# Eleven projection pairs in two transformer blocks: twelve half gates ahead of the pairs, the angle operations in three pairs, stores at the stage heads, transposes ahead of the last gate

## The reference

```python
h = modulate(rms_norm(x, g_pre_mix[l]), shift_m, scale_m)
proj = h @ w_in[l]
q_a, k_a, v_a, q_m, k_m, v_m, o_m, i_m, f_m, g_a, g_m = jnp.split(proj, split_points, axis=-1)
q_a = rope(q_a.reshape(B, S, N_Q_HEADS, HEAD_DIM), positions)
k_a = rope(k_a.reshape(B, S, N_KV_HEADS, HEAD_DIM), positions)
...
qk_m = jax.nn.silu(causal_depthwise_conv(jnp.concatenate([q_m, k_m], axis=-1), conv_w[l], conv_b[l]))
...
h_m = mlstm_chunkwise(q_m, k_m, v_m, i_pre, f_pre)
...
merged = jax.nn.sigmoid(g_a) * (y_a @ w_branch_attn[l]) + jax.nn.sigmoid(g_m) * (y_m @ w_branch_mlstm[l])
```

## Time and profile before

| what | us |
|---|---|
| median of 3 runs | 2745.44 (2743.47 to 2746.28) |
| the profiled execution, its own time | 2742.76 |
| its span (what the profile shows) | 2740.7 |
| PE busy in the span | 2645.3 |
| POOL busy, DVE busy, ACT busy | 1819.3, 1891.0, 1059.6 |
| mean granted TensorE clock, of full speed | 0.992 |

### The profile page before, as it was taken

The page is one execution under the profiler, slowest core; times in us unless marked ns, Lnnn a source line. Parts: engine busy times, 40 slices in busy tenths (PEclk is TensorE's granted clock), DMA queues, the critical chain, the costliest instruction groups (busy, mean ns, idle before and its releaser), DMA issues.

```text
span 2740.7 us, 39654 instructions
## 1 busy us (share of the span) xinstructions
PE 2645.3 (97%) x12718; PEld 2101.6 (77%) x12718; DVE 1891.0 (69%) x2671; ACT 1059.6 (39%) x2141; POOL 1819.3 (66%) x1389
## 2 busy tenths in 40 slices
PE   7999999899999999999899999999999999999998
PEld 5777777677788888877677787777887888888887
DVE  6666687738888888887776463485547667667667
ACT  5555444535534333333433233555234322222222
POOL 4555511357798888876679973222368898888874
PEclk9999999999999999999999999999999999999999
DMA  4322222034211111123422434222444111111133
GB/s 148 104 85 85 92 94 62 16 123 150 78 58 54 54 55 54 55 99 132 161 96 93 123 112 177 78 73 86 152 159 142 46 58 55 56 55 54 58 127 139
DMA packets 98697, 253.55 MB, mean 93 GB/s; under 512 B 9423, under 2 KB 13296, under 8 KB 98292
## 3 DMA queue, kind: packets, MB, share of 16 engines
q1 hardware_dynamic: 72464, 186.41, 21.2%
q10 hardware_dynamic: 26084, 65.21, 6.6%
HBM read 211.20 MB, written 37.77 MB: 91 GB/s over the span
## 4 chain that ended last, share of the span: by engine, by line
PE 82%; DVE 11%; ACT 3%; issue 3%; DMA 0%; ACTq 0%; POOL 0%; POOLq 0%; DVEq 0%; SPq 0%
PE ps L1260 9%; PE ps L1262 9%; PE ps L1261 9%; PE ps L1630 8%; PE ps L1632 8%; PE ps L1631 8%; PE ps L1677 4%; PE ps L1679 4%; PE ps L1678 4%; PE ps L1351 3%; PE ps L1841 2%; PE ps L1843 2%; PE ps L1842 2%; PE ps L1367 2%; PE ps L1937 1%
## 5 line engine op out<-in xcount | busy, mean ns | idle before, releaser
L935 POOL CAST wh<-raw 128x1024 fp32r<-128x1024 f32 x139 | 149.9, 1078 | 584.6 <-PE ps L1262 532.1
L1260 PE MATMUL ps<-hh,wh 128*128 128x512 f32 x1040 | 437.4, 421 | 22.7 <-DVE hl L3230 11.2
L1262 PE MATMUL ps<-hh,wl 128*128 128x512 f32 x1040 | 410.0, 394 | 0.0
L1261 PE MATMUL ps<-hl,wh 128*128 128x512 f32 x1040 | 408.5, 393 | 0.0
L937 POOL TENSOR_TENSOR wl<-raw,wh 128x1024 fp32r<-128x1024 f32 x139 | 336.0, 2417 | 11.1
L1050 POOL TENSOR_TENSOR wl<-raw,wh 128x512 fp32r<-128x512 f32 x156 | 212.7, 1378 | 72.5 <-ACT wh L2442 72.0
L1260 PEld LDWEIGHTS ps<-hh,wh 128*128 128x128 f32 x1040 | 197.3, 190 | 79.8 <-issue 15.0
L1262 PEld LDWEIGHTS ps<-hh,wl 128*128 128x128 f32 x1040 | 196.4, 189 | 43.6
L1261 PEld LDWEIGHTS ps<-hl,wh 128*128 128x128 f32 x1040 | 197.6, 190 | 35.8 <-issue 3.4
L3595 DVE TENSOR_TENSOR hlf<-ps,hlf 128x512 f32<-128x512 f32 x252 | 171.5, 691 | 23.9 <-PE ps L1679 21.7
L1631 PE MATMUL ps<-al,wh 128*128 128x512 f32 x476 | 185.2, 389 | 0.0
(11 more groups left out here) (463 smaller groups left out, 7289.3 us busy)
## 6 DMA issues: line engine op xcount, KB each, us to landing
raw<-weights SPq DMA_DIRECT2D x149, 512.0 KB, 3.6
raw<-weights SPq DMA_DIRECT2D x240, 256.0 KB, 2.6
arena<-w_ada SPq DMA_DIRECT2D x48, 512.0 KB, 3.8
arena<-gate_scratch ACTq DMA_DIRECT2D x25, 512.0 KB, 5.1
gate_scratch<-arena ACTq DMA_DIRECT2D x14, 512.0 KB, 2.8
gate_scratch<-sums_f ACTq DMA_DIRECT2D x17, 256.0 KB, 2.0
arena<-x_t ACTq DMA_DIRECT2D x1, 4096.0 KB, 14.2
x_scratch<-arena ACTq DMA_DIRECT2D x2, 2048.0 KB, 9.1
```

The source lines that it names most:

```text
L1260: pe.matmul(out, wh[:, slot, w], xh, start=start, stop=False)
L1261: pe.matmul(out, wh[:, slot, w], xl, start=False, stop=False)
L1262: return pe.matmul(out, wl[:, slot, w], xh, start=False, stop=stop)
```

## The change

`N_EARLY` becomes 12: one gate half moves from behind the pairs to ahead of them, with its strip, its chunk of weights and its split; strips 8 to 11 use the other half of their tiles and so wait for no earlier store. In pair 0, block 0 now comes before the first half of the rows. The positions are loaded behind the weights of pair 1 instead of ahead of them. POOL waits for all low parts of the activation sums before it starts the weights of pair 1. The angle operations are spread over pairs 1, 2 and 3, and ACT's two sines stand at the end of stage 4. `rope_store` of a pair's first tile stands at the head of its stage. Behind the pairs three gate halves are left; the stabilizer columns follow the first and use banks 5 and 4, all 40 transposes follow the second with three pairs of banks instead of two, and the third gate half comes last. ACT's load of `NEGMB` and its copies of the stabilizer columns are issued earlier, and the last eviction lies inside the recurrence's first step.

```diff
-N_QKV, N_WO, N_FFN, N_PROJ, N_GATE, N_EARLY, N_BR, N_OUT = 24, 14, 3 * NJ + 10, 23, 16, 11, 8, 16
+N_QKV, N_WO, N_FFN, N_PROJ, N_GATE, N_EARLY, N_BR, N_OUT = 24, 14, 3 * NJ + 10, 23, 16, 12, 8, 16
...
+        VT_BANKS = ((0, 1), (2, 3), (6, 5), (0, 1), (2, 3))
...
                 weights(C_PR + 1)
-                sp.wait_ge(Z.n_lo, 48)
-                sp.wait_ge(Z.gs5, 16 * N_EARLY)
-                sp.dma_start(TURNS.bitcast(I32), A.positions).then_inc(Z.pos_in, 16)
                 for j in range(1, N_PAIRS):
...
                     pr_load(j, 1, 1)
+                    if j == 1:
+                        sp.wait_ge(Z.n_lo, 48)
+                        sp.wait_ge(Z.gs5, 16 * N_EARLY)
+                        sp.dma_start(TURNS.bitcast(I32), A.positions).then_inc(Z.pos_in, 16)
...
                 direct_low(0, 6, 0, b22)
+                pool.wait_ge(R.px_lo, PR_LOWS + 16)
                 for j in range(1, N_PAIRS):
...
                     pe.wait_ge(Z.g_ev, N_EARLY - 2)
+                    projection_block(j, 0, b, True)
+                    pe.wait_ge(Z.g_ev, N_EARLY)
                     rows_half(0)
-                    pe.wait_ge(Z.g_ev, N_EARLY)
-                    projection_block(j, 0, b, True)
                     pe.wait_ge(Z.n_lo, 48)
                     rows_half(1)
...
-                if m == N_EARLY + 1:
+                if m == N_EARLY:
+                    stabilizer_columns()
+                elif m == N_EARLY + 1:
                     pe.wait_ge(R.v_back, 16 * 5)
                     pe.wait_ge(Z.if_ev, N_PROJ - 1)
                     v_transposes(0)
                     pe.wait_ge(Z.if_ev, N_PROJ)
                     v_transposes(1)
-                elif m == N_EARLY + 2:
-                    v_transposes(2)
-                    v_transposes(3)
-            v_transposes(4)
-            stabilizer_columns()
+                    pe.wait_ge(Z.g_ev, N_EARLY + 1)
+                    pe.wait_ge(Z.m_tpc, 2)
+                    for n in range(2, 5):
+                        v_transposes(n)
             pe.wait_ge(Z.v_cp, 10)
...
             def projection_stage(j):
 
+                rope_store(j - 2, 0)
                 if j:
                     projection_out(j - 1, 0)
                 projection_copy(j)
                 if j:
                     projection_out(j - 1, 1)
                 projection_cast(j, 2)
-                rope_store(j - 2, 0)
                 row_steps(j)
-                if j == 4:
-                    act.wait_ge(Z.trig, 14)
-                    act.activation(SIN, SIN, ACT.Sin, scale=col("sgn")).then_inc(Z.trig_sin, 1)
-                    act.activation(COS, COS, ACT.Sin).then_inc(Z.trig_sin, 1)
...
                 rope_store(j - 2, 1)
+                if j == 4:
+                    act.wait_ge(Z.trig, 14)
...
+            act.wait_ge(Z.m_row, 16)
+            act.wait_ge(Z.cv_done, 6)
+            act.dma_start(NEGMB, bass.AP(m_dram.tensor, 0, [[0, P], [S, HD_ML], [1, S]])).then_inc(Z.m_mb, 16)
             projection_end(N_PAIRS - 1, 0)
             projection_end(N_PAIRS - 1, 1)
...
+            late_out(N_EARLY)
+            act.wait_ge(Z.m_tp, 4)
+            act.activation(GT, bank(5)[:, 0:32], ACT.Copy).then_inc(Z.m_tpc, 1)
+            act.activation(EMT, bank(4)[:, 0:32], ACT.Copy).then_inc(Z.m_tpc, 1)
+            late_out(N_EARLY + 1)
...
                 projection_add(j, bank(b + 3), bank(b + 2), PR_SUM7, 4, 2)
                 rope_turn(j - 1, 0)
+                if j == 1:
+                    angle_start()
+                elif j == 2:
+                    angle_whole()
+                elif j == 3:
+                    angle_turns(0.25)
                 projection_add(j, bank(b + 1), bank(b + 1), PR_SUM, 5, None)
+                if j == 1:
+                    angle_turns(0.0)
+                elif j == 2:
+                    angle_part(SIN, C1, ANGLE)
+                elif j == 3:
+                    angle_whole()
                 projection_add(j, bank(b + 2), bank(b + 2), PR_SUM, 6, 3)
...
-                if j == 2:
-                    angles(SIN, 0.0)
-                if j == 3:
-                    angles(COS, 0.25)
+                angle_steps(j)
```

More of the change, by code:

```diff
@@ L447, in taps_done @@
             return T_CV[-1] * group + T_CV[2 * u + p]
-        E_STRIPS = [T(m % 8)[:, 0:HALF] for m in range(N_EARLY)]
+        E_STRIPS = [T(m % 8)[:, m // 8 * HALF:(m // 8 + 1) * HALF] for m in range(N_EARLY)]
         E_BANKS = (7, 0, 1, 4)
@@ L1476, in v_transposes @@
                 for half in range(2):
-                    if n >= 2:
-                        pe.wait_ge(Z.v_cp, 2 * (n - 2) + half + 1)
+                    if n >= 3:
+                        pe.wait_ge(Z.v_cp, 2 * (n - 3) + half + 1)
                     for b in range(4):
                         t = slice(half * HALF + b * P, half * HALF + (b + 1) * P)
-                        last = pe.transpose(bank(2 * (n % 2) + half)[:, b * P:(b + 1) * P], V_BACK[n][:, t], mat("ident"))
+                        last = pe.transpose(bank(VT_BANKS[n][half])[:, b * P:(b + 1) * P], V_BACK[n][:, t], mat("ident"))
                     last.then_inc(Z.vT, 1)
@@ L1886, in stabilizer_columns @@
                 pe.wait_ge(Z.if_act, 4)
-                pe.wait_ge(Z.v_cp, 8)
                 for b in range(NB):
-                    pe.matmul(bank(2)[:, b * 4:b * 4 + 4], ROW1[0:4, b * P:(b + 1) * P], mat("ident")[0:4, 0:4],
+                    pe.matmul(bank(5)[:, b * 4:b * 4 + 4], ROW1[0:4, b * P:(b + 1) * P], mat("ident")[0:4, 0:4],
                               start=True, stop=True)
-                    last = pe.matmul(bank(3)[:, b * 4:b * 4 + 4], ROW2[32:36, b * P:(b + 1) * P],
+                    last = pe.matmul(bank(4)[:, b * 4:b * 4 + 4], ROW2[32:36, b * P:(b + 1) * P],
                                      mat("ident")[32:36, 32:36], start=True, stop=True)
@@ L2849, in projection_stage @@
                 rope_store(j - 2, 1)
+                if j == 4:
+                    act.wait_ge(Z.trig, 14)
+                    act.activation(SIN, SIN, ACT.Sin, scale=col("sgn")).then_inc(Z.trig_sin, 1)
+                    act.activation(COS, COS, ACT.Sin).then_inc(Z.trig_sin, 1)
             projection_copy(0)
@@ L2868, in _, with late_out @@
             act.preload_act_table_set("natural_log_exp_and_others")
-            for m in range(N_EARLY, N_GATE - 1):
-                strip_out = (Z.gs0, Z.gs1, Z.gs2, Z.gs3)[m - N_EARLY]
+            def late_out(m):
+                i = m - N_EARLY
                 act.wait_ge(Z.chunk_done, C_GATE0 + m + 1)
-                if m == N_EARLY + 2:
+                if i == 2:
                     act.wait_ge(Z.cv_done, 5)
-                act.activation(G_STRIPS[m - N_EARLY], bank(G_BANKS[m - N_EARLY]), ACT.Copy).then_inc(Z.g_ev, 1)
+                act.activation(G_STRIPS[i], bank(G_BANKS[i]), ACT.Copy).then_inc(Z.g_ev, 1)
                 act.wait_ge(Z.g_ev, m + 1)
-                act.dma_start(sg_dram[HD_ML + m][:, half_of(0)], G_STRIPS[m - N_EARLY]).then_inc(strip_out, 16)
-                if m == N_EARLY:
-                    act.wait_ge(Z.m_row, 16)
-                    act.wait_ge(Z.cv_done, 6)
-                    act.dma_start(NEGMB, bass.AP(m_dram.tensor, 0, [[0, P], [S, HD_ML], [1, S]])).then_inc(Z.m_mb, 16)
+                act.dma_start(sg_dram[HD_ML + m][:, half_of(0)], G_STRIPS[i]).then_inc((Z.gs0, Z.gs1, Z.gs2)[i], 16)
+            late_out(N_EARLY)
[3 more added lines that the diff above has]
+            late_out(N_EARLY + 1)
             act.wait_ge(Z.vT, 10)
@@ L2885, in _ @@
                 act.dma_start(ROPE_HOME[r], sg_dram[25 + r]).then_inc(R.rope_back, 16)
-            act.wait_ge(Z.m_tp, 4)
-            act.activation(GT, bank(2)[:, 0:32], ACT.Copy).then_inc(Z.m_tpc, 1)
-            act.activation(EMT, bank(3)[:, 0:32], ACT.Copy).then_inc(Z.m_tpc, 1)
             def gate_out(c):
@@ L3000, in _ @@
                         m_weights(ML_QUARTERS[s][t])
+                    if (s, t) == (0, 0):
+                        late_out(N_EARLY + 2)
+                    if (s, t) == (1, 0):
+                        for strip_out in (Z.gs0, Z.gs1, Z.gs2):
+                            act.wait_ge(strip_out, 16)
                     if t and 0 <= s - 1 < ML_N:
@@ L3997, in _ @@
                     dve.tensor_copy(V2[:, 4 * half:4 * half + 4, o:o + P],
-                                    bank(2 * (n % 2) + half).rearrange("p (b n) -> p b n", b=4)).then_inc(Z.v_cp, 1)
-            dve.wait_ge(Z.chunk_done, C_GATE1 - 1)
+                                    bank(VT_BANKS[n][half]).rearrange("p (b n) -> p b n", b=4)).then_inc(Z.v_cp, 1)
             def m_diag(s):
```

43 lines of the change are left out of this document (22 added, 21 removed).

## The result

The changed kernel takes 2728.85 us (median of 6 runs, 2727.34 to 2735.85), the kernel before beside it 2745.86 (2741.59 to 2748.2, 6 runs). The ratio is 0.9945, with a 95% interval from 0.9931 to 0.9959 (a gain of 11 to 19 us). The forecast was 2728.8. The profiled execution took 2728.0, its span 2725.9.

The account below looks back on a forecast made before the run. PE was taken as the bound, busy 97% of the span. The terms 7.9 + 6.7 - 4.0 + 4.4 + 1.6 = 16.6, taken from the median 2745.44, gave 2728.8 us; range 2722.5 to 2737.5.

Parts of the forecast that it names:

- Pair 0: In pair 0, one more gate half ahead covers DVE's sums; PE waits 0 to 0.5 us; gain 7.9.
- Angles, stall gone: In pair 3, spreading the angle operations removes PE's stall on DVE's sums; gain 6.7.
- POOL late next: In pairs 3 and 4, PE newly waits on POOL's splits; loss 4.0 in short pieces, bounds 1.6 and 7.5.
- the rule of the Trainium skill: In pairs 3 and 4, DVE and POOL lock the SBUF ports for whole instructions; new wait 5.1 instead of 4.0.
- Rope stores: In pair 7, issuing the first rotated head's store sooner removes the 4.70 loss; 0.3 kept for POOL, gain 4.4.
- the term's lower bound: For the rope stores in pair 7, gain only 0.8 if POOL has no more than 0.8 spare.
- Behind the pairs: From the last pair to the first scores, ACT's wait goes and weights cost 0.2; gain 1.6, bounds 0.5 and 1.9.

Follow-up runs that it names:

- Run 12: The kernel before with only twelve gate halves ahead and, in pair 0, block 0 ahead of both rows halves; 2736.9 us, ratio 0.9969.
- run 11: The changed kernel once more, the same program; 2728.34 us, ratio 0.9935.
- run 7: The changed kernel with both the angle operations in two blocks and the rope store back where they were; 2729.26 us, ratio 0.9946.
- angles of 8 columns (8): The changed kernel with its fourteen angle operations and two sines working on 8 of 1024 columns, order and waits kept; 2724.21 us, ratio 0.9924.
- run 9: The changed kernel with ACT casting blocks 1 and 4 from pair 3 on, earlier in its queue, without POOL's wait ahead of pair 1; 2724.48 us.
- run 10: The kernel of run 9 with the angle operations back in two blocks of seven; 2728.88 us, ratio 0.9936.
- run 3: The changed kernel with the angle operations back in two blocks of seven, behind pairs 2 and 3; 2731.63 us, ratio 0.9947.
- run 2: The changed kernel without POOL's wait for the last low parts ahead of pair 1; 2727.33 us, ratio 0.9934.
- runs 5 and 6: The changed kernel with ACT casting blocks 1 and 4 from pair 2 on; 2731.74 us with POOL's wait ahead of pair 1, 2732.97 without.

## Why the prediction was right, and where it was right by luck

The total was right: 16.6 us forecast against 17.0 in the medians (15.1 by the ratio, 11 to 19 by its interval), 13.3 in the stretches of the one profile. Step by step:

- **Pair 0.** Forecast 7.9 and a wait under 1 us. Measured: 132 matmuls in 30.08 (30.17 by the measure), no wait, 8.2 won. Run 12 shows that the gain stands alone. Right.
- **Angles, stall gone.** No wait on DVE's sums is left in pair 3. Right as a row.
- **POOL late next.** Forecast 4.0, a first part in pair 3 and the rest in pair 4, in pieces short of 2.78 and without a fall of the clock. Measured: 3.71 + 0.97 = 4.7 lost, waits of 1.86 and 0.69 and some 1.7 at the lower clock. The mechanism and the pairs are right, most of it came sooner than said, and the clock fell after less idleness than the earlier trace rows had shown. By the rule of the Trainium skill that the prediction weighed ("SBUF — State Buffer", section "SBUF: two separate sides", an exclusive lock) it would have been 5.1. The total doesn't decide between 4.0 and 5.1: without the fall of the clock, in run 11, pairs 3 and 4 lost 4.5. The rows speak for the rule in kind: two casts of POOL's that began inside DVE's scans (scans over 4 gate rows, L3942 and L3947) took 2.61 instead of 0.61 and ended 0.42 and 0.41 after the scan, which is a wait and no sharing. The wait goes both ways, which the prediction left out: each scan ended 2.14 or 2.15 after the end of the POOL operation in whose time it had begun, so of its 3.3 us some 1.1 were its own wait.

```profile
1445.72 3.28 DVE L3942 TENSOR_TENSOR_SCAN arena<-arena 4x1024 f32<-4x1024 f32 x1
1449.04 1.45 DVE L3944 TENSOR_TENSOR arena<-arena 4x1024 f32<-4x1024 f32 x1
1450.52 3.27 DVE L3947 TENSOR_TENSOR_SCAN arena<-arena 4x1024 f32<-4x1024 f32 x1
...
1444.70 2.16 POOL L1157 TENSOR_TENSOR weight_sum<-raw,weight_sum 128x512 f32<-128x512 f32 x1
1446.81 2.61 POOL L1147 CAST wh<-arena 128x512 fp32r<-128x512 f32 x1
1449.49 2.15 POOL L1149 TENSOR_TENSOR wl<-arena,wh 128x512 fp32r<-128x512 f32 x1
1451.59 2.61 POOL L1147 CAST wh<-weight_sum 128x512 fp32r<-128x512 f32 x1
1454.28 1.29 POOL L1149 TENSOR_TENSOR wl<-weight_sum,wh 128x512 fp32r<-128x512 f32 x1
```

Before, where the first scan began later in POOL's operation, it took 2.58, and again ended 2.14 after that operation:

```profile
1450.78 2.58 DVE L3927 TENSOR_TENSOR_SCAN arena<-arena 4x1024 f32<-4x1024 f32 x1
...
1449.61 1.61 POOL L1145 CAST wh<-arena 128x512 fp32r<-128x512 f32 x1
```

- **Rope stores.** Forecast 4.4. The 4.70 of pair 7 went, but a wait of 1.93 on POOL in pair 8 took 1.7 back, net 3.0. This is the term's lower bound at work (POOL busy for 23.08 of 23.90), of which I had kept only 0.3.
- **Behind the pairs.** Forecast 1.6 and a stretch of 22.7. Measured 24.42, a gain of -0.1, as some nine matmuls behind the small ones ran at the lower clock; in five other profiles the stretch was 22.83 or 22.84. PE waited for nothing there, and the weights of the last half were in time. Work and waits as forecast, the clock not.

What the runs show to be wrong is how the sum gives the gains to the edits. It prices the spread angles at 6.7 - 4.0 = 2.7 and the rope store at 4.4, 7.1 together. The four kernels that have one, both or neither (pairs in us) say:

| | store at the head | store where it was |
|---|---|---|
| angles spread | 228.95 | 229.15 |
| angles in blocks | 227.92 | 229.50 |

Both together are worth 0.55 (two profiles of the same pairs differ by 0.2). With the angles in blocks the store alone brings 1.58, and spreading the angles on top takes 1.03 of that away. The failed step is "Here too POOL was busy 23.08 of 23.90, so I keep 0.3 for it", and the like in the angles: each stall was priced as if POOL's lateness arose and ended beside it. POOL's lateness is one account over pairs 1 to 8. The times by which its low part for block 1 was ready ahead of that block's first matmul (from the timelines of POOL and PE; 0.05 is a wait):

| pair | 2 | 3 | 4 | 5 | 6 | 7 | 8 | 9 |
|---|---|---|---|---|---|---|---|---|
| after | 4.4 | 0.05 | 1.0 | 0.7 | 2.8 | 1.4 | 0.05 | 2.3 |
| both moves undone (7) | 4.8 | 1.2 | 3.2 | 1.0 | 3.2 | 1.6 | 2.3 | 2.7 |
| angles of 8 columns (8) | 4.8 | 1.2 | 2.1 | 4.2 | 5.4 | 3.4 | 2.0 | 2.5 |

With small angles, the gate rows take 3.6 of the lead (4.8 to 1.2), the rotations 3.4 (5.4 to 2.0), and a pair without either gives back up to 2.1 (2.1 to 4.2). The full angle operations take 8.2 by pair 5: ready 0.7 ahead with PE 4.7 late, against 4.2 ahead with PE on time. With small ones the lead never ends, and pair 8 waits for nothing. With full ones it ends in pair 3 or, if DVE's stall there gives POOL time, nearly does; and what is late in pair 4 is still missing in pair 8. So a stall removed from DVE comes back as a wait on POOL until POOL has less to do. Runs 9 and 10 show the other side: with two casts on ACT the same spreading is worth 3.96. Both these kernels also lack POOL's hold, and the wait on DVE's sum is 4.07 in run 10 against 2.83 in run 3, so not all of the 3.96 need be due to the casts.

Where, then, did the profile's gain in pairs 1 to 10 come from (204.10 to 198.87)? Run 12 has none of it, run 7, with both moves undone, has 4.7 of the 5.2: pair 3 took 24.46 for 25.93, pair 7 21.36 for 23.90, and pairs 5 and 8 lost nothing. What is left in run 7 beside pair 0 is POOL's hold, the later positions, the later sines and the part behind the pairs. The prediction priced these at nothing within the pairs. PE's waits became 2.1 shorter in all, and most of the other 2.6 is clock: in pair 7 the starts behind the wait (1.82, before 2.78) stayed at the full clock, where before seven of them had stood 0.43 apart, and in pair 3 it was seven instead of eleven.

The waits on DVE's sums (2.83 for 3.98, 1.82 for 2.78) are shorter because DVE itself lost less time to POOL. In pair 3 the gate rows and the seven angle operations took 15.4 us before and 14.8 in run 7; in pair 6 the first product of a rotation, ahead of the sum that ACT copies before it can issue the store, took 2.35 before and 1.65 in run 7:

```profile
1545.92 2.35 DVE L3884 TENSOR_TENSOR arena<-arena 128x1024 f32<-128x1024 f32 x1
...
1540.68 1.65 DVE L3887 TENSOR_TENSOR arena<-arena 128x1024 f32<-128x1024 f32 x1
```

Which edit does it is not settled. The chain of pair 3 took 14.7 to 14.8 in the two kernels with POOL's hold and the angles in blocks (runs 3 and 7), and 15.4 to 15.5 in the three without the hold (before, runs 10 and 12). Run 10 has the later positions and the later sines, so these two alone don't shorten it. The hold, which sets POOL 0.6 later against PE (run 2), is the likely cause, but run 10 also has its casts on ACT, and no run changes the hold alone in such a kernel.

So that the sum met the total is in part luck: it gave the two moves 7.1 where they brought 0.6, and the unpriced edits nothing where they brought 4.7; the rest of the difference is the clock behind the pairs and what the profile and the medians differ by.

## What to carry to other kernels

When an engine is busy for 97% of a stretch (POOL here, 25.12 of 25.93), a stall of the engine that it serves (PE here) in that stretch is its slack: keep one account of its lead over all stages that follow, and don't price each stall by itself. Before removing such a stall, take work off the nearly full engine; spreading the angles was worth -1.0 us without two casts moved and +4.0 us with them (and without POOL's hold). And an operation handed to another engine must stand in its queue ahead of anything that waits later than the receiver needs it: against the kernels without them, the same two casts lost 3.0 and 6.1 us (runs 5 and 6) behind the first copy of the stage and won 3.9 at the places of run 9 (against run 2), which also left out pair 2.
